# Down projections of a decoder trunk in five rounds of half-size block products

## Chip, cores and metric

The kernel runs on one core of one Trainium2 chip. The metric is the device time of one execution in microseconds (us), lower is better; it is the median of several runs. Two versions of the kernel are compared on the same chip. The engines are named as in the profile: PE is the matrix engine (TensorE), DVE the vector engine, ACT the scalar engine, POOL the GpSimd engine, SP the engine whose queue issues most DMAs. SBUF is the on-chip memory, PSUM the eight accumulator banks of PE.

## What is computed

The reference is a decoder trunk of two layers on one sequence of 1024 tokens and 1024 features: a short-convolution layer, then a layer of dilated attention over shared keys and values. Each layer ends with a gated feed-forward block of inner size 2816, and each part is normed before and after:

```python
def _swiglu(x, w_in, w_out):
    gate, up = jnp.split(x @ w_in, 2, axis=-1)
    return (jax.nn.silu(gate) * up) @ w_out

for layer in range(DEPTH):                       # DEPTH = 2
    g = norm_g[layer]
    xn = _rms_norm(x, g[0])
    if layer < N_A:
        mix = _short_conv(xn, conv_in_w[layer], conv_w[layer], conv_out_w[layer])
    else:
        if shared is None:
            shared = _shared_kv(x, kv_norm_g, kv_w)
        mix = _dilated_attention(xn, q_w[j], o_w[j], shared, slopes)
    x = x + _rms_norm(mix, g[1])
    ff = _swiglu(_rms_norm(x, g[2]), ffn_in_w[layer], ffn_out_w[layer])
    x = x + _rms_norm(ff, g[3])
```

The change concerns `(...) @ w_out`, the down projection: 1024 tokens by 2816 inner features times 2816 by 1024, once in each layer. All data is float32.

## The kernel before

**Precision.** PE multiplies in a rounded format, so each float32 factor is split into a high and a low part: ACT copies it with rounding (`*_hi`), DVE subtracts that from the original (`*_lo`). A product is three matmuls: high x high, high x low, low x high.

**Phases.** They follow each other as `PHASES` lists them: `conv_in`, `conv_out`, `norm1`, `up0`, `down0`, `norm2`, `attn`, `oproj`, `norm3`, `up1`, `down1`, `norm4`. Each engine has one program, written out by hand in its order; semaphores (`Signal` objects, one count for each phase) let engines wait for each other. There is no scheduler: an instruction that waits holds up everything behind it on its engine.

**Up projection (`up0`, `up1`).** It already computes each pair of column blocks as seven products of sums of blocks. For each of 22 sets POOL makes four sums of weight blocks (L1971), ACT and DVE split them (L1083, L1506), PE runs 7 products of 12 matmuls of 128x512 (L741), and DVE adds the results out of the banks. The inner features go to DRAM (`hid_spill`).

**Down projection (`down0`, `down1`).** The inner features are 22 tiles of 128. A unit is one tile `f` and one half of the tokens; the first 22 units serve tokens 0 to 511, the second 22 the rest. For each unit SP loads a 128x1024 block of `ffn_out_w` (`raw`, two buffers) and a 128x512 block of features back from DRAM (`hraw`). ACT and DVE split both (`w_hi`/`w_lo`, L1017 and L1400; `h_hi`/`h_lo`, L1185 and L1605). PE adds the unit to four token tiles, each in two banks: 4 x 2 x 3 = 24 matmuls (L770), 1056 in a layer. POOL has nothing to do for a unit.

**Norms.** After unit 22 the four token tiles of the first half are taken out of the banks: ACT squares them (L1065), DVE multiplies by the gain (L1472), POOL makes the inverse root (L1892, L1898), ACT scales and POOL and DVE add to the residual (L1118, L1935, L1480). This happens in `down_layer` between units of the second half. The last two units are done tile by tile, so that the norm of the second half starts with its first tile. After `down0`, in phase `norm2`, the normed tiles (`xn`, L1493) are transposed by PE (L639) and split (L1028, L1412) as the input of attention. POOL scales the first weight chunks of attention by the norm's gain (L1995).

The few lines of PE that the change replaces, in `down_layer`:

```python
passes = [(n, a, w) for n in units
          for a, w in ((h_hi, w_hi), (h_hi, w_lo), (h_lo, w_hi))]
for h in range(2):
    for i, (n, a, w) in enumerate(passes):
        mm = pe.matmul(bank(b + h), a[:, n % SPLIT_RING, t % HT * P:(t % HT + 1) * P],
                       w[:, a_slot(base + n), h * HALF:(h + 1) * HALF], ...)
```

## Time and profile before

| | us |
|---|---|
| median of 3 runs | 2508.31 |
| lowest and highest | 2507.82, 2512.53 |
| span of the profiled execution | 2505.2 |
| first down projection, about | 236.5 (844.5 to 1081.0) |
| from there to attention's last input | 25.9 (1081.1 to 1107.0) |
| second down projection, about | 239.1 (2257.5 to 2496.6) |
| end of the last down projection to the end | 8.6 |

How to read the profile: it is one execution. Busy time of an engine is the time in which it works on an instruction; a group of instructions is named by its line in the code, its engine, what it writes and reads, and its shape. "Idle before" an instruction is put down to what released it. Matmuls overlap in PE, so the time of a single one is longer than the distance to the next. In a row of the timeline the first number is the start and the second the duration; if another engine or a lock holds an instruction up after it has begun, that is inside its duration.

### The profile page before, as it was taken

How to read it: one execution, taken by the hardware profiler on the slowest of the kernel's cores; microseconds unless marked ns; L12 is line 12 of the kernel's file. 1: busy time of each engine (PE TensorE's matmuls, PEld its weight loads, DVE VectorE, ACT ScalarE, POOL GpSimd, SP SyncE). 2: the span in 40 equal slices, each digit the busy share in tenths (PEclk: the TensorE clock that was granted, in tenths of full speed). 3: DMA queues.
4: the chain of work that ended last, by engine and by line, in shares of the span. 5: the costliest groups of instructions: out<-in, count | busy, mean ns of one | idle time of the engine just before them, and what ended most of it. 6: DMA issues, size and time to landing. Idle time of an engine off the chain costs nothing.

```text
span 2505.2 us, 31211 instructions
## 1 busy us (share of the span) xinstructions
PE 2341.8 (93%) x10928; PEld 1939.1 (77%) x10928; DVE 1297.0 (52%) x1962; ACT 907.6 (36%) x1692; POOL 477.2 (19%) x542
## 2 busy tenths in 40 slices
PE   7999996999999999988898889879889999999998
PEld 5888784888888888866777777767668888888887
DVE  4333319655665434374555555563485565553443
ACT  3111116323232234343555555563442232332333
POOL 1000018222222001031111111100552222210011
PEclk9999997999999999999999999999889999999999
DMA  4111111233223444442323222222023223324444
GB/s 135 44 49 50 59 42 43 76 87 90 76 76 93 130 144 148 143 141 70 70 57 75 62 60 55 68 51 110 25 68 100 78 76 89 89 69 168 142 148 146
DMA packets 202209, 219.28 MB, mean 88 GB/s; under 512 B 13792, under 2 KB 153056, under 8 KB 200032
## 3 DMA queue, kind: packets, MB, share of 16 engines
q1 hardware_dynamic: 199136, 206.10, 28.1%
q10 hardware_dynamic: 2944, 11.53, 1.3%
q8 instruction: 72, 1.18, 0.2%
q14 instruction: 57, 0.47, 0.1%
HBM read 160.98 MB, written 31.46 MB: 77 GB/s over the span
## 4 chain that ended last, share of the span: by engine, by line
PE 84%; DVE 6%; ACT 3%; issue 3%; POOL 3%; DMA 1%; SPq 0%; DVEq 0%; ACTq 0%; POOLq 0%
PE banks L741 33%; PE banks L770 19%; PE banks L600 11%; PE banks L842 8%; PE banks L681 6%; PE banks L880 2%; PE banks L892 2%; PE banks L905 2%; POOL raw L1995 1%; PE banks L919 1%; ACT w_hi L1017 1%; DMA q_stack<-q_parts 1%; DVE w_lo L1400 1%; PE banks L639 1%; ACT scores L1349 1%
## 5 line engine op out<-in xcount | busy, mean ns | idle before, releaser
L741 PE MATMUL banks<-xb,up_split 128*128 128x512 f32 x3696 | 848.5, 392 | 11.9 <-DVE xb L1449 11.9
L741 PEld LDWEIGHTS banks<-xb,up_split 128*128 128x128 f32 x3696 | 699.8, 190 | 158.2 <-issue 12.4
L1400 DVE TENSOR_TENSOR w_lo<-raw,w_hi 128x1024 fp32r<-128x1024 f32 x152 | 188.2, 1239 | 434.1 <-ACT w_hi L1017 432.4
L1017 ACT CAST w_hi<-raw 128x1024 fp32r<-128x1024 f32 x152 | 159.1, 1049 | 451.2 <-PE banks L770 290.1
L770 PE MATMUL banks<-w_hi,h_hi 128*128 128x512 f32 x704 | 273.9, 389 | 0.0
L770 PE MATMUL banks<-w_hi,h_lo 128*128 128x512 f32 x704 | 273.9, 389 | 0.0
L770 PE MATMUL banks<-w_lo,h_hi 128*128 128x512 f32 x704 | 273.9, 389 | 0.0
L1506 DVE TENSOR_TENSOR up_split<-sums,up_split 128x512 fp32r<-128x512 f32 x176 | 154.1, 877 | 163.5 <-ACT up_split L1083 163.3
L1971 POOL TENSOR_TENSOR sums<-raw_up 128x512 f32<-128x512 f32 x88 | 115.1, 1310 | 395.9 <-DMA raw_up<-in_ffn_in_w 197.8
L770 PEld LDWEIGHTS banks<-w_hi,h_lo 128*128 128x128 f32 x704 | 132.1, 188 | 27.7
L770 PEld LDWEIGHTS banks<-w_hi,h_hi 128*128 128x128 f32 x704 | 132.1, 188 | 27.4
L770 PEld LDWEIGHTS banks<-w_lo,h_hi 128*128 128x128 f32 x704 | 132.1, 188 | 27.2
L1802 DVE TENSOR_TENSOR pt<-banks,pt 128x128 fp32r<-128x128 f32 (+7 forms) x128 | 96.9, 757 | 100.7 <-ACT pt L1293 100.0
L1083 ACT CAST up_split<-sums 128x512 fp32r<-128x512 f32 x176 | 108.5, 618 | 88.4 <-PE banks L741 86.9
L2031 POOL TENSOR_TENSOR resid<-o_parts 128x64 f32 (+1 forms) x128 | 46.9, 366 | 480.9 <-ACT o_parts L1309 480.9
L842 PE MATMUL banks<-x_hi,w_hi 128*128 128x512 f32 x384 | 112.6, 411 | 10.3 <-DVE x_lo L1412 6.2
L1506 DVE TENSOR_TENSOR up_split<-raw_up,up_split 128x512 fp32r<-128x512 f32 x132 | 116.4, 883 | 7.7 <-ACT up_split L1083 7.7
L842 PE MATMUL banks<-x_lo,w_hi 128*128 128x512 f32 x384 | 119.9, 413 | 0.0
L1786 DVE CUSTOM_DVE_ANT_0 scores<-banks,bias 128x128 f32<-128x128 f32 (+7 forms) x128 | 96.5, 754 | 36.9 <-PE banks L880 33.3
L880 PE MATMUL banks<-k_stack,q_stack 128*128 128x256 f32 (+1 forms) x382 | 94.2, 355 | 22.8 <-DVE neg_max L1786 13.3
L842 PE MATMUL banks<-x_hi,w_lo 128*128 128x512 f32 x384 | 114.1, 410 | 0.0
L1349 ACT ACTIVATE scores<-scores,neg_max 128x128 f32<-128x128 f32 (+7 forms) x128 | 99.8, 780 | 19.9 <-DVE neg_max L1786 19.5
(146 smaller groups left out, 3349.8 us busy)
## 6 DMA issues: line engine op xcount, KB each, us to landing
raw_up<-in_ffn_in_w SPq DMA_DIRECT2D x88, 512.0 KB, 5.4
raw<-in_ffn_out_w SPq DMA_DIRECT2D x88, 512.0 KB, 3.5
hid_spill<-hid SPq DMA_DIRECT2D x88, 256.0 KB, 2.5
hraw<-hid_spill SPq DMA_DIRECT2D x88, 256.0 KB, 3.5
k_stack<-k_parts SPq DMA_DIRECT2D x32, 512.0 KB, 6.3
raw<-in_conv_in_w SPq DMA_DIRECT2D x24, 512.0 KB, 3.8
raw<-in_kv_w SPq DMA_DIRECT2D x16, 512.0 KB, 3.9
q_stack<-q_parts SPq DMA_DIRECT2D x64, 128.0 KB, 2.3
```

What stands on the lines that cost most here:

```text
L600: mm = pe.matmul(bank(out_bank), w[:, slot, k * P:(k + 1) * P], a[:, k, h * HALF:(h + 1) * HALF], start=(i == 0), stop=(i == len(passes) - 1))
L681: mm = pe.matmul(bank(t), a(2 * q + k)[:, t * P:(t + 1) * P], w[:, slot, k * HALF:(k + 1) * HALF], start=(q == 0 and i == 0), stop=(last a ...
L741: mm = pe.matmul(bank(b_out), up_split[:, p, a, q * P:(q + 1) * P], xb[:, RIGHT_OF[p], b, q, :], start=(i == 0), stop=(i == len(passes) - 1))
L770: mm = pe.matmul(bank(b + h), a[:, n % SPLIT_RING, t % HT * P:(t % HT + 1) * P], w[:, a_slot(base + n), h * HALF:(h + 1) * HALF], start=(n ...
L842: mm = pe.matmul(bank(PROJ + h), w[:, a_slot(chunk0["attn"] + c), k * P:(k + 1) * P], a[:, k, h * HALF:(h + 1) * HALF], start=(i == 0), st ...
L880: mm = pe.matmul(psum[:, SCORE + lo // HALF, 0:hi - lo], att["q_stack"][:, e, i * P:(i + 1) * P], att["k_stack"][:, e, n, lo:hi], start=(n ...
L1017: act.copy(w_hi[:, a_slot(n), :], raw[:, s, :]).then_inc(hi_ready.sem, 1)
L1083: act.copy(up_split[:, p, 0, :], src).then_inc(up_hi.sem, 1)
L1349: act.activation(att["scores"][:, s % 2, 0:n], att["scores"][:, s % 2, 0:n], ACT.Exp, bias=neg_max[:, s % 2:s % 2 + 1], scale=-1.0, accum_ ...
L1400: dve.tensor_tensor(w_lo[:, a_slot(n), :], raw[:, n % RAW_RING, :], f32(w_hi[:, a_slot(n), :]), ALU.subtract) \
L1506: dve.tensor_tensor(up_split[:, p, 1, :], src, f32(up_split[:, p, 0, :]), ALU.subtract).then_inc(up_lo.sem, 1)
L1971: pool.tensor_tensor(sums[:, out_, :], a, b, op).then_inc(summed.sem, 1)
```

## The change

Two tiles of inner features, `2m` and `2m+1`, form a pair; there are 11 pairs. With the two halves of the tokens and the two halves of the output features a pair is a 2x2 by 2x2 block product, and the new code computes it as seven products of 128x512 sums instead of eight. In each product A is a sum or difference of feature blocks (128 features x 512 tokens), B one of weight blocks (128 x 512), and PE adds 4 token tiles x 3 matmuls = 12 of 128x512 into four banks. A layer has 77 products, in five rounds:

| round | products | sums on POOL | sums on DVE | banks |
|---|---|---|---|---|
| 1, q = 0 to 21 | M3, M5 in turn | 1 each | none | 0 to 3, 4 to 7 |
| 2, q = 22 to 43 | M1, M4 in turn | 2 for M1 | 1 for M4 | the same |
| 3, q = 44 to 54 | M7 | 1 | 1 | 4 to 7 |
| 4, q = 55 to 65 | M2 | 1 | none | 4 to 7 |
| 5, q = 66 to 76 | M6 | 2 for even q, 1 for odd | 1 for odd q | 0 to 3 |

Each product is made in a fixed order: sums (POOL and DVE, `block_sums`, `right_sum`) into one of two buffers `down_sums`; rounding (ACT, `split_high`); subtraction (DVE, `split_low`) into one of three buffers `down_split`; then PE. POOL's sum for product q waits until DVE has split product q-2, ACT's rounding until PE has done product q-3. Where both factors are sums, ACT and DVE treat them as one operation of 1024 columns, otherwise as two of 512.

Between the rounds the banks are read. ACT copies M3, M5 and M1 out; DVE adds M4, M7, M2 (twice) and M6 to the four result blocks in `acc_tile`; POOL adds up C12 in SBUF. The first half's tokens are complete after round 3, and their norm is laid between the products of rounds 4 and 5. In the first layer their transposes, splits and the first scaled chunk of attention weights are laid there too; before, the transposes came at the end of the phase. The last three products are run tile by tile, once all three are split.

The inner features are loaded back from DRAM once for each block and stay in SBUF (`hid_tile`). Weights come as 128x512 blocks into 12 buffers (8 in round 5). Some attention buffers have other addresses. The up projection is unchanged except in its last set, where the first splits of the down projection stand.

The diff, cut to its core:

```diff
+    def product(self, q):
+        n = self.pairs
+        if q < 2 * n:
+            return (M3, M5)[q % 2], q // 2
+        if q < 4 * n:
+            return (M1, M4)[q % 2], (q - 2 * n) // 2
+        if q < 6 * n:
+            return (M7, M2)[q // n - 4], q % n
+        return M6, 7 * n - 1 - q
...
+    def pool_makes(self, q):
+        p, m = self.product(q)
+        return (1, 1, 2, 0, 1, 1, 2 - m % 2)[p]
+
+    def dve_makes(self, q):
+        p, m = self.product(q)
+        return (0, 0, 0, 1, 1, 0, m % 2)[p]
...
+                def tile_product(q, i):
...
+                    side = down_split[:, q % DOWN_RING]
+                    passes = ((0, 0), (0, 1), (1, 0))
+                    for j, (a, b) in enumerate(passes):
+                        mm = pe.matmul(bank(b_out), side[:, a, 0, i * P:(i + 1) * P], side[:, b, 1, :],
+                                       start=(p in (M3, M5, M1, M2) and first and j == 0),
+                                       stop=(last and j == len(passes) - 1), skip_group_check=True)
...
+                pe.wait_ge(*down_lo.at(ph, 2 * QN))
+                for i in range(HT):
+                    for q in range(QN - 3, QN):
+                        tile_product(q, i)
...
+                for q in range(DOWN_RING, QN):
+                    right_sum(ph, q + 1)
+                    split_low(ph, q)
+                    for t in range(HT):
+                        if q == 44:
+                            add_m4(t)
+                        elif q == 56:
+                            sum_c11(t)
+                        elif q == 67:
+                            add_m2(t)
+                        if q == 60 + t:
+                            gain_first(t)
+                        if q == 62 + t:
+                            right_added(norm_ph, t)
+                        if pre and q == (72, 73, 75, 76)[t]:
+                            low_part(norm_ph, t)
+                    if pre and q == 74:
+                        prepare(chunk0["attn"])
...
+                for q in range(QN):
+                    block_sums(ph, q)
+                    for t in range(HT):
+                        if q == 25:
+                            sum_c12(t)
+                        if q == 60 + t:
+                            inverse_root(square1, mean1, rstd1, t, sq1_done, mean1_done, rstd1_done,
+                                         norm_ph)
+                        if q == 63 + t:
+                            left_added(norm_ph, t)
```

**DVE in the middle of the down projection.** Before, for units of the second half: `raw` and `hraw` are the loaded weights and features.

```order
L1400 TENSOR_TENSOR w_lo<-raw,w_hi 128x1024
L1605 TENSOR_TENSOR h_lo<-hraw,h_hi 128x512
L1480 SCALAR_TENSOR_TENSOR resid<-acc,rstd,resid 128x640
L1400 TENSOR_TENSOR w_lo<-raw,w_hi 128x1024
L1605 TENSOR_TENSOR h_lo<-hraw,h_hi 128x512
```

Now, at the end of round 4 and the start of round 5 (`down_sums` is a sum, `down_split` its split, `acc_tile` a result block):

```order
L1855 TENSOR_TENSOR down_split<-down_sums_89,down_split 128x512
L1857 TENSOR_TENSOR down_split<-down_raw,down_split 128x512
L1710 SCALAR_TENSOR_TENSOR resid<-acc_tile_81,rstd,resid 128x640
L1967 TENSOR_TENSOR acc_tile_83<-acc_tile_83,g_post 128x1024
L1855 TENSOR_TENSOR down_split<-down_sums_88,down_split 128x512
```

```order
L1860 TENSOR_TENSOR down_split<-down_sums_89,down_split 128x1024
L1950 TENSOR_TENSOR acc_tile_84<-banks,acc_tile_84 128x512
L1954 TENSOR_TENSOR acc_tile_84<-acc_tile_84,banks 128x512
L1950 TENSOR_TENSOR acc_tile_85<-banks,acc_tile_85 128x512
L1954 TENSOR_TENSOR acc_tile_85<-acc_tile_85,banks 128x512
L1950 TENSOR_TENSOR acc_tile_86<-banks,acc_tile_86 128x512
L1954 TENSOR_TENSOR acc_tile_86<-acc_tile_86,banks 128x512
L1950 TENSOR_TENSOR acc_tile_87<-banks,acc_tile_87 128x512
L1954 TENSOR_TENSOR acc_tile_87<-acc_tile_87,banks 128x512
L1871 TENSOR_TENSOR down_sums_89<-down_raw 128x512
L1860 TENSOR_TENSOR down_split<-down_sums_88,down_split 128x1024
```

The gain and the reads of the banks stand now between splits that PE waits for, and sums stand among them.

**POOL during the norm of the first half.** Before:

```order
L1935 TENSOR_TENSOR resid<-resid,acc 128x384
L1892 TENSOR_SCALAR mean<-square 128x1
L1898 TENSOR_TENSOR rstd<-mean,neg_half 128x1
```

Now, at the same work (end of round 4, start of round 5; `hid_tile` is a block of inner features):

```order
L2251 TENSOR_TENSOR resid<-resid,acc_tile_82 128x384
L2300 TENSOR_TENSOR down_sums_88<-hid_tile_78 128x512
L2303 TENSOR_TENSOR down_sums_88<-down_raw 128x512
L2208 TENSOR_SCALAR mean<-square 128x1
L2214 TENSOR_TENSOR rstd<-mean,neg_half 128x1
L2251 TENSOR_TENSOR resid<-resid,acc_tile_83 128x384
L2300 TENSOR_TENSOR down_sums_89<-hid_tile_76 128x512
```

POOL's sums for the products stand now between the operations of the norm.

## Rows read from the trace of the kernel before

**Rows 1.** The page: span, busy time and share by engine, and the chain by engine.

```profile
span 2505.2 us, 31211 instructions
...
PE 2341.8 (93%) x10928; PEld 1939.1 (77%) x10928; DVE 1297.0 (52%) x1962; ACT 907.6 (36%) x1692; POOL 477.2 (19%) x542
...
PE 84%; DVE 6%; ACT 3%; issue 3%; POOL 3%; DMA 1%; SPq 0%; DVEq 0%; ACTq 0%; POOLq 0%
```

**Rows 2.** Windows: length, busy of PE, PEld, DVE, ACT, POOL; clock, DMA share, GB/s.

```profile
844.50:1081.00 236.50, 236.50 (x1045) 195.76 (x1044) 96.69 (x104) 79.48 (x110) 16.25 (x26) 1.00 0.44 147
1081.00:1106.00 25.00, 17.89 (x101) 14.65 (x99) 20.56 (x19) 16.66 (x24) 10.93 (x17) 0.93 0.09 28
2257.50:2496.60 239.10, 239.10 (x1056) 197.83 (x1055) 95.37 (x101) 75.90 (x104) 12.43 (x20) 1.00 0.44 149
2496.60:2505.20 8.60, 0.24 (x2) 0.00 (x0) 5.29 (x4) 2.23 (x4) 3.68 (x5) 0.65 0.53 215
426.00:844.00 418.00, 418.00 (x1835) 345.85 (x1836) 253.31 (x350) 127.34 (x223) 112.45 (x90) 0.99 0.28 83
```

**Rows 3.** Groups of the page: busy us, mean ns of one, idle before.

```profile
L770 PE MATMUL banks<-w_hi,h_hi 128*128 128x512 f32 x704 | 273.9, 389 | 0.0
```

**Rows 4.** Timeline of the up projection: start us, duration us, engine, line, operation.

```profile
611.33 1.29 POOL L1971 TENSOR_TENSOR sums<-raw_up 128x512 f32<-128x512 f32 x1 [3.43 <-DVE up_split L1506]
611.77 1.40 DVE L1506 TENSOR_TENSOR up_split<-sums,up_split 128x512 fp32r<-128x512 f32 x1
...
441.89 1.30 POOL L1971 TENSOR_TENSOR sums<-sums,raw_up 128x512 f32<-128x512 f32 x1 [0.63 <-DVE up_split L1506]
442.00 0.69 DVE L1658 TENSOR_TENSOR third_gate<-third_gate,banks 128x512 f32<-128x512 f32 x1 [0.19 <-PE banks L741]
```

**Rows 5.** Timeline where DVE and POOL both have work queued.

```profile
427.80 1.73 POOL L1971 TENSOR_TENSOR sums<-raw_up 128x512 f32<-128x512 f32 x1
428.31 1.77 DVE L1506 TENSOR_TENSOR up_split<-raw_up,up_split 128x512 fp32r<-128x512 f32 x1
429.49 1.73 POOL L1971 TENSOR_TENSOR sums<-raw_up 128x512 f32<-128x512 f32 x1
...
411.32 1.28 POOL L1942 TENSOR_TENSOR xb<-t,xb 128x512 fp32r<-128x512 f32 x1
411.72 1.97 DVE L1489 SCALAR_TENSOR_TENSOR xn<-resid,rstd,g_pre 128x1024 f32<-128x1024 f32 x1
```

**Rows 6.** Timeline of the first down projection, during the first half's norm.

```profile
977.34 1.01 POOL L1935 TENSOR_TENSOR resid<-resid,acc 128x384 f32<-128x384 f32 x1 [13.78 <-ACT acc L1118]
977.40 1.50 DVE L1605 TENSOR_TENSOR h_lo<-hraw,h_hi 128x512 fp32r<-128x512 f32 x1
```

**Rows 7.** Durations of the operations, ns min/median/max, with first and last start.

```profile
L1400 DVE TENSOR_TENSOR w_lo<-raw,w_hi x152: 1214/1225/2772, 19.7 to 2481.7; 128x1024 fp32r<-128x1024 f32 x152
L1506 DVE TENSOR_TENSOR up_split<-sums,up_split x176: 676/687/1783, 402.3 to 2240.3; 128x512 fp32r<-128x512 f32 x176
...
L1017 ACT CAST w_hi<-raw x42: 1043/1048/1054, 853.2 to 1073.1; 128x1024 fp32r<-128x1024 f32 x42
```

**Rows 8.** DMAs of the down windows: KB and us to landing; GB/s in 40 slices.

```profile
hraw<-hid_spill SPq DMA_DIRECT2D x42, 256.0 KB, 3.5
...
GB/s 214 234 213 132 132 139 154 172 163 165 133 133 133 132 132 141 154 157 179 154 100 175 132 132 132 139 145 171 162 171 125 145 132 132 132 138 343 136 0 69
```

**Rows 9.** Timeline of `norm1`: a power of one column on POOL and DVE's addition.

```profile
376.00 0.55 POOL L1898 TENSOR_TENSOR rstd<-mean,neg_half 128x1 f32<-128x1 f32 x1
376.19 0.88 DVE L1480 SCALAR_TENSOR_TENSOR resid<-mix_conv,rstd,resid 128x640 f32<-128x640 f32 x1
```

**Rows 10.** Timeline of `norm2`, after PE's last down matmul.

```profile
1081.20 1.02 ACT L1065 ACTIVATE junk<-banks 128x1024 bf16<-128x1024 f32 x1 [1.10 <-PE banks L770]
...
1095.81 1.90 POOL L1995 TENSOR_TENSOR raw<-raw,gains 128x1024 f32<-128x1024 f32 x1
...
1105.75 1.22 DVE L1412 TENSOR_TENSOR x_lo<-banks,x_hi 128x1024 fp32r<-128x1024 f32 x1 [1.04 <-ACT x_hi L1028]
```

More of the change, by code:

```diff
@@ new lines, in load_ffn @@
+                    if n < FT - 1:
+                        store_hidden(up, n)
+                for m in range(NP - 4, NP):
+                    for i in range(2):
+                        load_block(down, layer, 2 * m + i, 2 * m + i, 1)
+                        load_hidden(layer, 2 * m + i, 2 * m + i, 1)
+                for m in range(NP):
+                    c = 2 * NP + 3 * m
+                    load_block(down, layer, c, 2 * m, 0)
+                    load_hidden(layer, c, 2 * m + 1, 2)
+                    load_block(down, layer, c + 1, 2 * m + 1, 1)
+                    load_block(down, layer, c + 2, 2 * m + 1, 0)
```

784 lines of the change are left out of this document (528 added, 256 removed).

## The prediction

> **What bounds the kernel now.** The page comes first: TensorE (PE) is busy for 93% of the span, and the chain of waits spends 84% in it [rows 1]. So a removed matmul counts in full, unless something else becomes late. Then the windows by stage: PE has no idle time in either down projection, and leaves it only after the first (25.0 us with 17.89 busy) and at the end [rows 2]. There 1045 matmuls take 236.50 us, 0.2264 us each; the 389 ns of a single one overlap [rows 2, 3]. VectorE (DVE) is busy for 40% of a down window and GpSimd (POOL) for 7%, so by busy shares alone all their new work would be hidden. The next view speaks against that.
>
> The timeline of the up projection shows DVE and POOL stopping each other. A DVE subtraction of 512 columns with both inputs in SBUF takes 0.69 us alone, and 1.40 us when it starts during a POOL operation: it ends 0.55 us after that one [rows 4, 7]. Beside the next POOL operation, a DVE operation that reads a PSUM bank keeps its 0.69 us [rows 4]. Where both engines have work queued they alternate, and one POOL and one DVE operation of 512 columns come every 1.69 us [rows 5]. I call what they share the port. It is held for 0.55 us by a DVE operation of 512 columns, 1.14 by a POOL one (1.69 - 0.55), and 1.09 by a DVE one of 1024 (411.72 + 1.97 = 413.69, 1.09 after POOL's end at 412.60) [rows 5]. So it is held some 0.13 us shorter than a DVE operation lasts alone, and 0.15 shorter than a POOL one. Before the change the port is lightly used in a down projection: 44 times 1.09 + 0.55 is 72 us of 239.
>
> **What is removed.** A layer has 1056 down matmuls, and after it 77 products of 12, 924. That is 132 x 0.2264 = 29.9 us a layer, **59.8 us** in all, if PE stays as full. One product lasts 12 x 0.2264 = 2.717 us.
>
> **What is added, round by round.** For each product both factors are split, and POOL and DVE make the sums. Port time against PE time:
> - M3 and M5, 11 pairs: 2 POOL sums and 4 DVE halves, 2 x 1.14 + 4 x 0.55 = 4.5 us of 5.43. Hidden.
> - M1 and M4, 11 pairs: 2.3 + 1.09 + 3 x 0.55 = 5.0 of 5.43. Hidden, but closely: POOL waits until the buffers of two products ago are split, and its queue also takes four sums of C12 at the round's start, 4 x 1.2 us. Bounds for both first rounds are 0 and 5 us a layer (0.4 for each pair if DVE's halves come ahead of POOL's sums); I take 2.
> - M7, 11 products: 1.14 + 0.55 + 1.09 = 2.78 us each, with the step from DVE's end to POOL's start (0.08) about 2.85, against 2.717. Ahead of it DVE adds four tiles from the banks, and behind it four more, before which M2 may not write: DVE takes them behind two further splits. I reckon 3 us lost (bounds 2 and 5).
> - M2, 11 products: 1.14 + 1.10 = 2.24, hidden at first, and DVE gets its lead of about 2.8 us back. From the sixth product on, the first half's norm is laid between them: four multiplications by the gain (1024 columns, now from SBUF and not from a bank, 1.09 each), four additions of 640 columns on DVE (0.88 alone, 0.75 held [rows 9]), four of 384 on POOL (1.01 alone, 0.86 held [rows 6]). I lay the queues beside each other, first come first served: from the split of the sixth product to that of the first M6 product 26.5 us pass (six splits, one sum on DVE and seven on POOL, which works two products ahead, and these twelve operations: 6.6 + 0.6 + 8.0 + 10.8 = 26.0, and the steps from engine to engine). PE has 16.3 us of work there and a lead of 3: 7 us lost.
> - M6, 11 products: six have two POOL sums, five one POOL and one DVE sum; a pair is 3 x 1.14 + 2 x 1.09 + 0.55 = 6.15 us against 5.43. I follow the queues. The second split comes 1.8 us behind the first. Then DVE takes eight operations of 512 columns from M2's banks (8 x 0.61 = 4.9 us), one sum (0.6) and the next split (1.15), while PE has 2.7 us of work: 4 us lost at one place. Four pairs at 5.9 to 6.3 us follow, since a sum must go POOL (1.29), ACT (1.05), DVE (1.22) before the next can start [rows 4, 7]. Last, PE runs three products tile by tile and starts when all three are split, 8.15 us. In all 1.8 + 6.7 + 24.4 + 8.15 = 41 us from the first product's start, against 11 x 2.717 = 29.9: 11 us lost (bounds 6 and 15).
>
> A layer therefore loses 2 + 3 + 7 + 11 = 23 us. The first layer adds a second norm in the same place: 1.9 us to scale a weight chunk on POOL, its split (1.09), and ACT's squares and scalings behind which the next split waits. DVE's four reads of the transposed tiles come from banks and fit in its waits. 5 us more (bounds 2 and 9). Reloading the inner features at the start may cost 0.5 us a layer: they land in 3.5 us [rows 8], PE needs them 8 us later. Sum **52 us**, bounds 20 and 75.
>
> **POOL's small operations, a rule weighed.** In the trace a power of one column takes 0.55 us on POOL, and a DVE addition that starts 0.19 us into it still takes 0.88 us [rows 9]; so I count its port time as nothing. The Trainium skill, page "SBUF — State Buffer", section "SBUF: two separate sides", says the shared pair is an exclusive lock held for the whole instruction. By that the twelve powers in these rounds would hold the port too, and the time would be 2500 and not 2493; the two rows of this case speak against it for so small an operation.
>
> **After the first down projection.** From PE's last down matmul (1081.1) to the last input of attention (1105.75 + 1.22 = 1107.0) pass 25.9 us [rows 10]. In that chain lie four splits of the first half's tiles and one chunk's scaling and splitting (1.90 + 1.05 + 1.22) [rows 7, 10]; the new code does these before PE ends. The second half's chain, down to the transposes that share banks, stays. I take **-6 us** (bounds -12 and 0), and -2 for two of four transposes that fall into PE's holes. At the very end the last tile's bank is read twice instead of once, in shorter operations, and tiles come every 2.04 instead of 2.72 us: **+0.5** on 8.6 us [rows 2].
>
> **Transfers.** A layer moves 154 blocks of 256 KB, 39 MB, in 209 to 235 us: 170 to 190 GB/s. The queues carry 147 at a share of 0.44, and 214, 234 and 343 GB/s in single slices of 6 us [rows 2, 8]. Twelve buffers cover some 11 us of lead against 3.5 us of landing. Hidden, at nothing; without that cover see rival B. The moved attention buffers change no instruction: nothing.
>
> **Sum.** The profiled execution has a span of 2505.2 us, 3.1 below the median of the runs. -59.8 + 52 - 8 + 0.5 = -15.3, so 2508.3 - 15.3 = **2493 us**.
>
> **Rivals.**
> - A, the port doesn't matter. For it: busy shares are low, and in the up projection DVE and POOL stop each other in every set of products while PE stays full [rows 2, 4], since products there wait with a lead. Against it: rounds M7 and M6 need more port time than PE time, and no lead survives eleven products. Time: all matmuls saved, with 0 to 20 us of loss: 2442 to 2470.
> - B, transfers become the bound and the kernel gets slower. Place: the rounds' loads, all in one queue. If they stayed at the 149 GB/s of now, a layer would take 39.4 MB / 149 = 264 us instead of 239, and the kernel 2508 + 50 - 8 = 2550. It decides from where less than 165 GB/s flows (39.4 / 239). The slices of 214 and more speak against it.
> - C, the waits chain worse than I follow. If DVE's halves always go ahead of POOL's sums, a pair in the first rounds needs 5.85 us, and M6 7 us or more: 65 to 75 us lost, 2506 to 2516.
> - D, POOL's powers hold the port for as long as they last, twelve times 0.55 us: 2493 + 6.6 = 2500. The addition of 0.88 us speaks against it [rows 9].
>
> **How the numbers follow.** Forecast 0.48 (2478 to 2503), D 0.10. A with the stretch up to 2478: 0.17. C: 0.17, of which three quarters lies within 0.2% of the time before and the rest above. B: 0.08. A measurement of this kernel can tell 0.2%, 5 us, from no change. Faster (below 2503.3): 0.48 + 0.10 + 0.17 less 0.03 for the upper edge of D, 0.72; within: 0.03 + 0.13 = 0.16; slower: 0.04 + 0.08 = 0.12. The range leaves out B and the lower half of A: 2462 to 2514.
>
> **What would show it.** Right: in the windows of the down projections PE has its idle time after the fourth product round starts, released by DVE's splits, some 20 us a layer; DVE's split of 1024 columns has a mean well above 1.22 us, and POOL's sums above 1.29; the first half of each window is full. The step at 1081 to 1107 is shorter by 6 us. Wrong: PE without idle time (A); POOL's or ACT's waits ended by loads of down_raw (B); idle time from the first round on (C). The weakest term is M6's 11 us, since it hangs on who goes first at the port.

## The result, and the profile after

The changed kernel takes **2557.95 us** (median of 4 runs, 2555.90 to 2559.78), the kernel before beside it 2508.07 us (median of 4). The ratio is 1.0191, with a 95% interval from 1.0177 to 1.0205: slower by 1.9%. The forecast was 2493 us, and its range ended at 2514. The profiled execution has a span of 2554.7 us against 2505.2 [rows 1].

The windows answer to [rows 2]. Columns are the stretch, its length, the busy time and instructions of PE, PEld, DVE, ACT and POOL, the granted clock, the DMA share and GB/s. The first six rows are the first down projection (rounds 1 to 4, round 5 up to its last three products, and those three), the seventh is the stretch behind it, and the last six are the second down projection.

```profile
844.90:914.10 69.20, 63.64 (x265) 51.48 (x265) 36.56 (x49) 29.34 (x52) 32.41 (x28) 0.95 0.60 206
914.10:982.00 67.90, 63.70 (x265) 48.39 (x264) 59.88 (x47) 24.29 (x35) 41.39 (x26) 1.00 0.46 155
982.00:1018.00 36.00, 33.03 (x133) 24.06 (x133) 34.56 (x28) 15.07 (x19) 20.44 (x13) 1.00 0.73 247
1018.00:1055.90 37.90, 32.69 (x132) 25.52 (x132) 31.87 (x31) 22.13 (x38) 30.91 (x27) 0.95 0.13 44
1055.90:1095.40 39.50, 29.17 (x129) 23.34 (x129) 29.38 (x27) 20.78 (x27) 32.69 (x23) 0.89 0.41 134
1095.40:1106.10 10.70, 10.70 (x37) 8.69 (x38) 6.17 (x8) 3.15 (x9) 7.89 (x11) 0.77 0.00 1
1106.10:1133.70 27.60, 15.54 (x57) 12.26 (x55) 15.39 (x17) 11.19 (x18) 11.68 (x16) 0.75 0.12 40
2290.00:2359.20 69.20, 62.72 (x266) 50.79 (x266) 36.46 (x49) 29.38 (x53) 31.95 (x24) 0.95 0.58 205
2359.20:2427.10 67.90, 63.65 (x266) 48.40 (x264) 59.86 (x47) 24.24 (x35) 41.38 (x26) 1.00 0.48 155
2427.10:2463.00 35.90, 32.88 (x132) 23.98 (x133) 34.45 (x28) 15.06 (x19) 20.36 (x13) 1.00 0.74 248
2463.00:2500.40 37.40, 32.40 (x132) 25.53 (x132) 32.99 (x31) 17.66 (x30) 29.35 (x23) 0.95 0.13 44
2500.40:2534.30 33.90, 23.05 (x97) 17.75 (x97) 26.19 (x22) 11.83 (x17) 26.55 (x17) 0.94 0.47 171
2534.30:2544.10 9.80, 9.80 (x36) 7.70 (x36) 4.80 (x7) 2.84 (x8) 7.85 (x10) 0.84 0.00 0
```

With PE full a round of 22 products takes 22 x 2.717 = 59.8 us and one of 11 takes 29.9. No round is full, and the loss begins in the first one. From PE's first to its last down matmul the first layer takes 261.2 us (full: 209.2) and the second 254.1; before, it was 241.3 and 239.5, read in the same way. The 49.5 us of difference between the spans lie as follows: first down projection +19.9, second +14.6, the stretch between them +12.2 (1171.7 to 1183.9), the end +2.2 (8.3 to 10.6), the start +0.6.

From the page of the changed kernel, the groups that answer to [rows 3]: PE's down matmuls, ACT's copy and DVE's subtraction of a whole product's sums (busy us, mean ns of one, idle time before and what ended it).

```profile
L964 PE MATMUL banks<-down_split 128*128 128x512 f32 x1848 | 454.6, 403 | 57.9 <-DVE down_split L1860 29.6
L1375 ACT CAST down_split<-down_sums 128x1024 fp32r<-128x1024 f32 x66 | 69.4, 1052 | 167.3 <-POOL down_sums L2291 77.9
L1860 DVE TENSOR_TENSOR down_split<-down_sums,down_split 128x1024 fp32r<-128x1024 f32 x66 | 113.1, 1713 | 30.5 <-ACT down_split L1375 30.1
```

PE stands for 57.9 us in the two layers together, where before it stood for none. DVE's operation of 1024 columns takes 1713 ns in the mean; before, one of this size had a median of 1225 [rows 7]. A chain can be read here: PE waits for DVE, DVE for ACT, ACT for POOL.

### Three places

**The start of the first round.** The waits of SP, in whose queue all loads stand (total, times, longest), and PE's idle times in the timeline:

```profile
SPq L558 <- DVE hid L1887: 11.9, 1, 11.9
```

```profile
848.53 3.02 PE L964 MATMUL banks<-down_split 128*128 128x512 f32 x12 [0.60 <-DVE down_split L1846]
852.36 5.73 PE L964 MATMUL banks<-down_split 128*128 128x512 f32 x24 [0.80 <-DVE down_split L1841]
862.25 5.06 PE L964 MATMUL banks<-down_split 128*128 128x512 f32 x11 [4.16 <-DVE down_split L1841]
```

The store of the last hidden tile (`store_hidden`, L558) stands in SP's queue after the second pair's loads. It waits 11.9 us for a tile that DVE multiplies only behind the first splits, and all loads from the third pair on stand behind it. PE runs dry three times, and the granted clock is at its half level, 1.2 GHz, from 861.4 on:

```profile
861.40:868.20 6.80, 5.95 (x14) 4.70 (x15) 5.46 (x6) 1.86 (x4) 4.40 (x3) 0.50 1.05 394
```

**Round 2.** The timeline of one pair M1 and M4 (start, duration; in brackets the idle time before and what ended it):

```profile
957.21 0.68 DVE L1850 TENSOR_TENSOR down_split<-hid_tile,down_split 128x512 fp32r<-128x512 f32 x1
957.46 1.57 POOL L2289 TENSOR_TENSOR down_sums<-hid_tile,hid_tile 128x512 f32<-128x512 f32 x1 [2.66 <-DVE down_split L1860]
957.81 1.77 DVE L1852 TENSOR_TENSOR down_split<-down_sums,down_split 128x512 fp32r<-128x512 f32 x1
959.00 1.74 POOL L2291 TENSOR_TENSOR down_sums<-down_raw 128x512 f32<-128x512 f32 x1
959.72 1.57 DVE L1871 TENSOR_TENSOR down_sums<-down_raw 128x512 f32<-128x512 f32 x1
960.84 1.05 ACT L1375 CAST down_split<-down_sums 128x1024 fp32r<-128x1024 f32 x1 [3.84 <-POOL down_sums L2291]
962.00 1.23 DVE L1860 TENSOR_TENSOR down_split<-down_sums,down_split 128x1024 fp32r<-128x1024 f32 x1 [0.72 <-ACT down_split L1375]
963.40 1.58 POOL L2289 TENSOR_TENSOR down_sums<-hid_tile,hid_tile 128x512 f32<-128x512 f32 x1 [2.66 <-DVE down_split L1860]
```

It is a ring: POOL's two sums (3.28 us from start to end, with two DVE operations taking turns at the port), ACT's copy 1.05, DVE's subtraction 1.23, and POOL again. From 957.46 to 963.40 pass 5.94 us; PE needs 5.43. POOL may not go ahead, since there are two buffers of sums and M1's is free only when it is split. POOL stands 2.66 us of each turn, and DVE waits .72 before its subtraction, so neither is full.

**Round 3.** One product M7:

```profile
988.59 0.69 DVE L1871 TENSOR_TENSOR down_sums<-down_raw 128x512 f32<-128x512 f32 x1
988.63 1.80 POOL L2294 TENSOR_TENSOR down_sums<-hid_tile 128x512 f32<-128x512 f32 x1 [1.26 <-DVE down_split L1860]
989.20 2.32 DVE L1860 TENSOR_TENSOR down_split<-down_sums,down_split 128x1024 fp32r<-128x1024 f32 x1
991.65 0.69 DVE L1871 TENSOR_TENSOR down_sums<-down_raw 128x512 f32<-128x512 f32 x1
```

The period is 3.06 us. DVE's sum holds the port to about 989.14 (.55), POOL's sum ends at 990.43 (1.29 later), DVE's split at 991.52 (1.09), and DVE starts again .13 later, because its next sum goes into the buffer that this split has just read and waits for the split's semaphore.

### The profile page after: what moved, and what is told of

The parts are those of the page before. It is cut to its first block, busy times and chain, and to the rows that moved or that the text cites. A ratio compares the mean times of both kernels' runs of the same rounds, so it can differ in the third digit from the quotient of the medians.

```text
span 2554.7 us, 31486 instructions
## 1 busy us (share of the span) xinstructions
PE 2322.6 (91%) x10664; PEld 1899.9 (74%) x10664; DVE 1490.2 (58%) x2118; ACT 956.2 (37%) x1802; POOL 782.1 (31%) x732
## 4 chain that ended last, share of the span: by engine, by line
PE 68%; DVE 11%; POOL 8%; issue 5%; ACT 5%; DMA 2%; SPq 0%; DVEq 0%; POOLq 0%; ACTq 0%
PE banks L913 32%; PE banks L764 10%; PE banks L1009 8%; PE banks L853 6%; PE banks L964 5%; DVE down_split L1860 3%; PE banks L1059 2%; PE banks L1047 2%; PE banks L1072 2%; ACT down_split L1375 1%; POOL down_sums L2291 1%; POOL down_sums L2289 1%; POOL raw_second L2401 1%; PE banks L1086 1%; POOL down_sums L2303 1%
## 5 line engine op out<-in xcount | busy, mean ns | idle before, releaser
L964 PE MATMUL banks<-down_split 128*128 128x512 f32 x1848 | 454.6, 403 | 57.9 <-DVE down_split L1860 29.6
L964 PEld LDWEIGHTS banks<-down_split 128*128 128x128 f32 x1848 | 351.2, 193 | 159.2 <-DVE down_split L1860 52.2
L1009 PE MATMUL banks<-x_hi,w_second 128*128 128x512 f32 x768 | 226.9, 414 | 5.7 <-ACT v_t L1507 3.3
L764 PE MATMUL banks<-x_hi,w_first 128*128 128x512 f32 x768 | 184.4, 392 | 7.8 <-DVE x_lo L1648 7.8
L764 PEld LDWEIGHTS banks<-x_hi,w_first 128*128 128x128 f32 x768 | 145.0, 189 | 38.4 <-issue 5.7
L1009 PEld LDWEIGHTS banks<-x_hi,w_second 128*128 128x128 f32 x768 | 138.4, 196 | 28.3 <-issue 6.3
L2117 DVE TENSOR_TENSOR pt<-banks,pt 128x128 fp32r<-128x128 f32 (+7 forms) x128 | 96.9, 757 | 100.4 <-ACT pt L1535 99.7
L1375 ACT CAST down_split<-down_sums 128x1024 fp32r<-128x1024 f32 x66 | 69.4, 1052 | 167.3 <-POOL down_sums L2291 77.9
L1860 DVE TENSOR_TENSOR down_split<-down_sums,down_split 128x1024 fp32r<-128x1024 f32 x66 | 113.1, 1713 | 30.5 <-ACT down_split L1375 30.1
L1009 PE MATMUL banks<-x_lo,w_second 128*128 128x512 f32 x384 | 120.9, 416 | 0.0
L1909 DVE TENSOR_TENSOR second_up<-first_up,banks 128x512 f32<-128x512 f32 x44 | 30.2, 687 | 138.1 <-PE banks L913 138.1
```

Of the source, the lines that this page charges most:

```text
L764: mm = pe.matmul(bank(out_bank), w_of[:, w, k * P:(k + 1) * P], a[:, k, h * HALF:(h + 1) * HALF], start=(i == 0), stop=(i == len(passes) - 1))
L964: mm = pe.matmul(bank(b_out), side[:, a, 0, i * P:(i + 1) * P], side[:, b, 1, :], start=(p in (M3, M5, M1, M2) and first and j == 0), stop ...
L1009: mm = pe.matmul(bank(PROJ + h), w_split(chunk0["attn"] + c)[:, w, k * P:(k + 1) * P], a[:, k, h * HALF:(h + 1) * HALF], start=(i == 0), s ...
L1860: dve.tensor_tensor(low, both[:], high, ALU.subtract).then_inc(down_lo.sem, 2)
L2117: dve.tensor_tensor(att["pt"][:, s % 2, 1, 0:n], two_banks(PROB)[:, 0:n], f32(att["pt"][:, s % 2, 0, 0:n]), ALU.subtract) \
```

## The experiments

Round times below go from the first matmul of a round to that of the next, in both layers (first / second). "Ratio" is to the kernel before, run beside each on the same chip (its median was 2511 to 2513 us in these sets); brackets are 95% intervals. Of each diff the core is shown; dots stand for the other lines.

| kernel | us, ratio | round 1 | 2 | 3 | 4 | 5 to the end |
|---|---|---|---|---|---|---|
| full PE | | 59.8 | 59.8 | 29.9 | 29.9 | 29.9 |
| changed | 2557.95, 1.0191 | 69.2 / 69.1 | 67.9 / 67.9 | 35.9 / 35.9 | 38.0 / 37.4 | 50.2 / 43.7 |
| later store | 2543.63, 1.0126 [1.0102, 1.0150] | 62.0 / 62.0 | 67.9 / 68.0 | 35.9 / 35.9 | 39.1 / 39.1 | 49.3 / 43.7 |
| third buffer | 2538.87, 1.0109 [1.0082, 1.0135] | 69.0 / 68.0 | 64.9 / 64.9 | 32.9 / 32.9 | 38.1 / 39.1 | 42.6 / 40.8 |
| tiny sums | 2496.66, 0.9934 [0.9913, 0.9955] | 66.3 / 65.1 | 59.8 / 59.8 | 30.7 / 30.7 | 30.2 / 30.5 | 43.6 / 37.5 |
| sums unread | 2537.79, 1.0102 [1.0072, 1.0133] | 68.8 / 66.2 | 62.0 / 62.4 | 35.8 / 35.7 | 37.5 / 39.0 | 46.3 / 43.4 |
| three edits | 2525.19, 1.0060 [1.0041, 1.0078] | 61.6 / 61.6 | 64.9 / 64.9 | 32.9 / 32.9 | 38.9 / 39.1 | 44.2 / 40.7 |
| and tiny norm | 2509.50 (one run) | 62.3 / 61.6 | 64.9 / 64.8 | 32.9 / 32.9 | 30.0 / 30.0 | 45.5 / 41.9 |
| DVE's sums | 2520.19, 1.0043 [1.0029, 1.0058] | 69.2 / 69.3 | 60.8 / 60.8 | 31.3 / 31.3 | 33.8 / 33.9 | 48.3 / 43.9 |
| with store, end | 2503.45, 0.9967 [0.9956, 0.9979] | 62.0 / 62.0 | 60.8 / 60.8 | 31.3 / 31.3 | 33.9 / 33.9 | 47.0 / 44.2 |

### The store in SP's queue

```diff
                             load_hidden(layer, 2 * m + 1, 2 * m + 1, 1)
-                            if m == 1:
+                            if m == 4:
                                 store_hidden(up, n)
```

> The changed kernel with one line moved: the last hidden tile's store (two DMAs that wait for the product of that tile) stands three pairs later in SP's queue. In the changed kernel SP waits 11.9 us in it (L558) with the loads of the third pair and later behind it, and PE stands .60, .80 and 4.16 us in the first round and runs 6.83 us at half clock after it. Theory that this head-of-line wait causes the first round's loss: round 1 falls from 69.2 us to 62 to 65 (full PE 59.8), both layers together give 8 to 14 us: 2544 to 2550. Rival, the queue's own speed or the sums pace round 1: it stays at 69 us and the time at 2556 to 2560.

Round 1 fell from 69.2 to 62.0 us in both layers, and the span by 13.1 us. The window shows the clock back at full and the queue no slower than before:

```profile
845.40:907.30 61.90, 60.56 (x264) 49.47 (x265) 44.13 (x49) 29.86 (x52) 35.19 (x28) 1.00 0.67 230
```

So the wait of 11.9 us behind the store costs 7.2 us a layer. It is one cause, with its size; by the medians the kernel gains 14.3 us, just more than the 8 to 14 expected.

### A third buffer for the sums

```diff
-        down_sums = [at(212, "down_sums0", [2, HALF]), at(40, "down_sums1", [2, HALF])]
+        down_sums = [at(212, "down_sums0", [2, HALF]), at(40, "down_sums1", [2, HALF]),
+                     at(44, "down_sums2", [2, HALF])]
...
-                both = down_sums[q % 2]
+                both = down_sums[q % 3]
...
-                    pool.wait_ge(*down_lo.at(ph, 2 * (q - 1)))
+                    pool.wait_ge(*down_lo.at(ph, 2 * (q - 2)))
```

> The changed kernel with a third buffer for the sums (44 KB, free there), so that POOL and DVE may write a sum two products ahead instead of one. Theory that a ring through two buffers (POOL sum, ACT copy, DVE low half, back to POOL) sets the pace of rounds 2 to 5: round 2 falls from 67.9 to 60 to 62 us, rounds 3 and 4 by 2 to 4 us each, both layers give 20 to 30 us: 2528 to 2538. Rival, the shared port: the same POOL and DVE work still has to pass it one after the other, round 2 stays above 66 us and the time at 2552 or more.

The time lies just past the ring theory's upper end, far from the rival's. But only a part of what it said of the rounds came true. Round 3 fell by 3.0 us as expected. Round 4 did not fall (38.1 and 39.1 us, where 2 to 4 us less were expected). Round 5 gained most, 7.6 us in the first layer and 2.9 in the second. Round 2 lost 5.1 us instead of 8.1 (expected: at most 2.2), and where it loses has changed. In its steady part POOL's first sum starts at 958.17 and 963.61, and PE has no idle time:

```profile
958.17 1.60 POOL L2290 TENSOR_TENSOR down_sums<-hid_tile,hid_tile 128x512 f32<-128x512 f32 x1 [1.60 <-DVE down_split L1853]
963.61 1.59 POOL L2290 TENSOR_TENSOR down_sums<-hid_tile,hid_tile 128x512 f32<-128x512 f32 x1 [1.60 <-DVE down_split L1853]
```

That is 5.44 us, PE's own pace. What is left is one gap at the round's start (and the clock behind it, 0.97 for the round), where POOL first makes the four C12 sums (7.46 us beside DVE's work), with further sums of M1 behind them in its queue:

```profile
914.65 7.46 POOL L2315 TENSOR_TENSOR acc_tile<-acc_tile,acc_tile 128x512 f32<-128x512 f32 x4 [1.24 <-ACT acc_tile L1415]
929.10 1.33 PE L965 MATMUL banks<-down_split 128*128 128x512 f32 x3 [3.15 <-DVE down_split L1861]
```

### Port or ring: sums of 8 columns, and sums that nobody reads

In the first kernel POOL's sums keep their places and waits and lose their length; in the second they keep length and place, but ACT doesn't wait for them (loads that overwrite what POOL reads wait for POOL instead).

```diff
+                w = slice(0, HALF if m == 0 else 8)
...
-                    pool.tensor_tensor(both[:, 0, :], hid_half(2 * m, 1), hid_half(2 * m + 1, 2), ALU.add) \
+                    pool.tensor_tensor(both[:, 0, w], hid_half(2 * m, 1)[:, w], hid_half(2 * m + 1, 2)[:, w], ALU.add) \
```

> The changed kernel with POOL's sums for the down products over 8 of 512 columns from the second pair of each round on (that part of the sums is left out). All waits and orders stay; POOL's use of the port and its share of the ring go. If the sums cause the rounds' loss in either way (port or ring), rounds 2, 3 and 4 come to within 2 us of full PE (59.8, 29.9, 29.9) and the time to 2470 to 2490. If the loads do, they stay as they are: 2550 or more.

```diff
-                both = down_sums[q % 2]
+                both = down_sums[q % 2] if m == 0 else own_sums
...
-                    act.wait_ge(*pool_sum.at(ph, plan.pool_sums(q)))
+                    if m == 0:
+                        act.wait_ge(*pool_sum.at(ph, plan.pool_sums(q)))
```

> The changed kernel with POOL's sums made in full but into a buffer that nobody reads, from the second pair of each round on (ACT and DVE split old contents: the sums are left out of the result), and ACT doesn't wait for them. The port carries all that it carried, the ring through POOL is cut. Port theory: rounds stay as they are, 2545 to 2558. Ring theory: rounds 2 to 4 within 2 us of full PE, as with tiny sums: 2470 to 2495.

```profile
911.20:971.00 59.80, 59.80 (x265) 49.54 (x264) 41.23 (x47) 24.91 (x35) 14.34 (x25) 1.00 0.57 182
971.00:1001.80 30.80, 30.26 (x134) 24.59 (x133) 22.44 (x27) 14.14 (x19) 7.61 (x12) 1.00 0.81 276
1001.80:1032.00 30.20, 30.12 (x132) 24.62 (x133) 25.38 (x31) 22.43 (x40) 18.89 (x26) 1.00 0.17 55
```

```profile
913.50:975.40 61.90, 60.60 (x265) 49.10 (x264) 59.58 (x47) 25.41 (x35) 42.03 (x26) 1.00 0.53 170
975.40:1011.20 35.80, 32.83 (x134) 23.97 (x133) 32.90 (x28) 14.83 (x19) 20.18 (x13) 1.00 0.75 249
1011.20:1048.70 37.50, 32.58 (x133) 25.84 (x134) 31.97 (x32) 23.08 (x40) 31.89 (x27) 0.95 0.13 45
```

The first fence is of the kernel with tiny sums (rounds 2, 3, 4): PE is full in round 2 and within .8 us of it in the others, with up to 276 GB/s from the queue. So POOL's sums, by port or ring, cost 61 us of the 97 that the two layers lose, and the loads cost nothing in these rounds. The time of 2496.7 is 7 us above what was expected (2470 to 2490); rounds 1 and 5 stay long, and round 5 still loses 13.7 and 7.6 us. The second fence is of the kernel with unread sums, whose time fell between the theories, and the rounds say why. Round 2 is a **ring**: cut it and 5.9 of 8.1 us come back, though DVE is as busy as before (59.58 us against 59.88). In rounds 3 and 4 nobody waits for POOL's sums any more, and they stay at 35.8 and 37.5: what holds them passes through the **port**. But in round 3 the port isn't alone. DVE's own sum still goes into one of two buffers here, and its period is 3.06 us as in the changed kernel. In the kernel with the third buffer it is 2.84, since the next sum starts before the split has ended:

```profile
990.89 0.68 DVE L1872 TENSOR_TENSOR down_sums<-down_raw 128x512 f32<-128x512 f32 x1
993.73 0.68 DVE L1872 TENSOR_TENSOR down_sums<-down_raw 128x512 f32<-128x512 f32 x1
```

So of the 6.0 us that round 3 loses, DVE's wait for its own buffer is 2.4 (11 times .22), the port's excess over PE's 2.717 us is 1.4, and 2.3 are the gap before round 4. With tiny sums the round takes 30.7 us: without POOL's time on the port, DVE's wait fits beside PE's work.

### The three edits together, and the norm in round 4

The third edit puts the first normalised tile behind the last C22 sum on DVE. In the changed kernel's timeline DVE stands 2.59 us at it, and the sum behind it, whose products PE ended at 1106.1, comes at 1110.56:

```profile
1106.62 0.68 DVE L1974 TENSOR_TENSOR acc_tile<-acc_tile,g_post 128x512 f32<-128x512 f32 x1
1109.89 0.75 DVE L1723 TENSOR_SCALAR acc_tile<-resid,rstd 128x1024 f32<-128x1024 f32 x1 [2.59 <-POOL rstd L2214]
1110.56 0.68 DVE L1961 TENSOR_TENSOR acc_tile<-banks,acc_tile 128x512 f32<-128x512 f32 x1
```

```diff
-                    if pre and i >= 2:
-                        normed(norm_ph, HT + i - 2)
+                    if pre and i >= 3:
+                        normed(norm_ph, HT + i - 3)
                 if pre:
+                    normed(norm_ph, TT - 2)
                     normed(norm_ph, TT - 1)
```

> The changed kernel with the later store, the third sums buffer, and one DVE step moved in the first down projection's end: the first normalised tile of the lower half (it waits for its root) stands behind the last tile's C22 sum instead of ahead of it; in the changed kernel DVE stood 2.59 us at that step with the sum behind it, whose bank was ready 4.5 us before. Late store gave 14 us and the third buffer 19 to 20 us by themselves. If they add up and the moved step gives 2 to 4 us: 2516 to 2524. If the late store's gain is eaten by the later rounds (what is loaded sooner is not needed sooner): 2528 to 2538. The stretch from the last down matmul to the last x_lo, 27.7 us in the changed kernel, should be 23.5 to 26 us.

It came 1.2 us above the first range. By the spans the two edits give 13.1 and 17.8 us, the moved step 3.1 of its stretch, and all three 35.8. By the medians it is 14.3 and 19.1, and 32.8 for all three. Within the scatter of some us they add up. The stretch from the last down matmul to the last `x_lo` fell from 27.5 to 24.4 us.

> The three edits, and of the norm's steps on the upper half of the tokens (rounds 4 and 5) the gain (DVE, 1024 columns), the right addition (DVE, 640) and the left addition (POOL, 384) cut to few columns: left out of the result. In full they take 4 x (1.21 + .87 + 1.09) = 12.7 us of DVE and POOL per layer. Theory that rounds 4 and 5 are bound by what DVE and POOL do one after the other on the port: they lose 8 to 12 us per layer together, 2498 to 2508. Rival, that they wait for the sums' ring or the squares' order: under 4 us per layer, 2514 or more.

Round 4 fell from 38.9 and 39.1 to 30.0 us: its whole loss is the upper half's norm and POOL's sums for M2 beside each other. 9 us come back there; round 5 takes 1.2 to 1.3 back, as its own work is no shorter, so a layer gains 6.9 and 8.0 us, at or just below the lower end of what was expected (8 to 12), and the one run of 2509.5 us lies 1.5 us above its range. With tiny sums, where the norm is full, round 4 is as short (30.2 and 30.5): either of the two by itself would fit, and only both together don't.

### The sums on DVE

```diff
-        return (1, 1, 2, 0, 1, 1, 2 - m % 2)[p]
+        return (1, 1, 0, 0, 0, 0, 0)[p]
...
-        return (0, 0, 0, 1, 1, 0, m % 2)[p]
+        return (0, 0, 2, 1, 2, 1, 2)[p]
```

The first line counts the sums that POOL makes for M3, M5, M1, M4, M7, M2, M6, the second DVE's; `right_sum` makes the left sum too where POOL has none.

> The changed kernel with the sums of rounds 2 to 5 all made by DVE, none by POOL; nothing else differs. A 128x512 sum takes DVE .55 to .68 us and POOL 1.09 to 1.30 us, and with nothing of POOL's beside them DVE's operations should all run at their undisturbed length: 4.5 us for a pair of round 2 (5.43 at full PE), 2.5 us for M7 and M6, 2.0 us for M2 (2.72). If the loss is POOL's time on the port and the ring through it: round 2 60 to 61 us, round 3 30.5, round 4 32 to 34, round 5 with the last three 36 to 40, 2510 to 2522. Rival, that DVE, now with all the work in one order, waits for ACT's copies in turn and becomes the bound: round 2 over 64 us and 2540 or more.

> The kernel with DVE's sums, and the later store and the moved step of the end. If all three add up: 2492 to 2504, a tie with the kernel before or faster. If DVE is the bound in rounds 2 to 5: 2522 or more.

The windows of the second kernel, rounds 2, 3, 4, 5 up to the last three:

```profile
907.00:967.80 60.80, 60.10 (x266) 49.44 (x265) 52.86 (x67) 24.97 (x35) 7.17 (x4) 1.00 0.56 180
967.80:999.10 31.30, 30.38 (x133) 24.53 (x132) 29.20 (x39) 14.08 (x18) 0.00 (x0) 1.00 0.75 257
999.10:1033.00 33.90, 31.15 (x133) 24.48 (x133) 32.20 (x42) 23.72 (x42) 16.12 (x19) 1.00 0.18 62
1033.00:1069.90 36.90, 27.87 (x128) 22.11 (x128) 36.33 (x41) 19.60 (x25) 14.52 (x10) 0.95 0.44 143
```

DVE does 20 operations more in round 2 and is busy for 7 us less (52.86, before 59.88): it no longer waits at the port inside them. Rounds 2 to 4 came within .8 us of what was expected, round 5 did not (48.3 and 43.9 us, expected 36 to 40). Its row says why for the first layer: DVE is busy for 36.33 of 36.90 us, so it is mostly DVE's own work that bounds it: 11 products of .60 + .60 + 1.14, eight additions from banks, and in the first layer four `x_lo` tiles and a weight split. With the later store and the moved step this is **faster than the kernel before**, by a third of a per cent: 2503.45 us, ratio 0.9967.

### What is left in rounds 4 and 5

Four more kernels build on that one: the first two on it, the third on the second, and the last has all edits.

```diff
-                    right_sum(ph, q + 1)
+                    right_sum(ph, q + 2)
```

> The kernel with DVE's sums, later store and moved end step, and with it the third sums buffer, DVE making its sums two products ahead instead of one. With DVE's sums round 2 came to 60.8 us, round 3 to 31.3, round 4 to 33.9, round 5 with the last three to 46.6 and 43.8. Theory that DVE's own busy time is what is left: nothing to gain, within 2 us of 2503. Rival, that DVE still waits for ACT's copies between a sum and its split: rounds 4 and 5 fall by 2 us or more each and the time to 2490 to 2497.

2499.94 us, ratio 0.9956 [0.9942, 0.9970]. Rounds 4 and 5 together went from 80.9 and 78.1 to 79.2 and 75.5 us. So both theories fell short: it is more than nothing, less than the rival's price.

```diff
-                        elif q == 56:
+                        elif q == 55:
                             sum_c11(t)
...
-                        if pre and q == (72, 73, 75, 76)[t]:
+                        if pre and q == (72, 73, 76, 76)[t]:
                             low_part(norm_ph, t)
-                    if pre and q == 74:
+                    if pre and q == 76:
                         prepare(chunk0["attn"])
```

> The kernel with DVE's sums, later store and moved end step; two more orders on DVE: in the first down projection the last two x_lo tiles of the upper half and the split of the next weights, three operations of 1.14 us, stand behind the last split instead of ahead of it (DVE stood 2.83 us idle there, waiting for PE); and the four C11 sums at the end of round 3 stand one split earlier. If DVE is the bound of rounds 4 and 5, the last split comes 2 to 3.4 us earlier in the first layer, and the gap at the start of round 4 (about 2.3 us in the changed kernel) closes to under 1 us in both layers, but what DVE gains there it also needs: 2498 to 2502 in all. If PE's end is set elsewhere: 2503 as before.

2501.09 us, 0.9959 [0.9946, 0.9972]. Round 3 fell from 31.3 to 30.6 us, and the first layer's round 5 from 47.0 to 43.8. Of those 3.2 us the stretch behind took 2.1 back (24.5 to 26.6 us to the last `x_lo`): the moved operations are needed there.

```diff
-                for q in range(QN - 3):
+                for q in range(QN - 2):
...
-                    for q in range(QN - 3, QN):
+                    for q in range(QN - 2, QN):
```

> As the kernel before it in this set, with the last two products instead of the last three computed tile by tile. Tile by tile, the PE starts only when the last split is there, so 8.15 us of matmul lie behind that split; with two it is 5.43 us, and the first tile is ready .68 us sooner. If the end is set by that PE work, 2 to 3 us less per layer: 2493 to 2497. If the norm's chain behind it (about 2.9 us of DVE and POOL per tile) sets the end, .5 to 1.5 us less per layer: 2497 to 2500.

2498.91 us, 0.9954 [0.9937, 0.9971]. The down projections end 1.4 and 4.2 us sooner, and what follows them takes 2.2 and 2.0 us longer (to the last `x_lo` 28.8 us; the end 12.6 instead of 10.5). The norm's chain, not PE's last tiles, sets the end. Three kernels show it in a row. PE finishes a last tile every 2.72 us before, 2.04 with three products and 1.36 with two, and the end takes 8.3, 10.5 and 12.6 us: three steps of .68 us (2.04) that PE gains come back behind it. In the changed kernel DVE's last three additions stand 2.95 and 2.92 us apart (2543.37, 2546.32, 2549.24), slower than PE's tiles.

> All that gave something: DVE's sums in rounds 2 to 5 with the third buffer and two products ahead (2499.9 by itself), the later store, the moved end step, the two orders on DVE and the last two products tile by tile (2498.9). If the third buffer's gain (1.5 to 3 us) is of the same waits as that of the last two products, nothing is added: 2497 to 2500. If they add up: 2493 to 2497. In either case faster than the kernel before by .5 to .8%.

2499.52 us (2496.72 to 2501.89), 0.9954 [0.9939, 0.9969]: nothing is added, as the first case said. The chain behind the products, DVE's own work and the first round's 1.8 us are what the rounds still show.

## Why the prediction was wrong

Term by term, both layers together. "Saved" is against the 480.8 us that the two down projections took before; 1.7 us of them are the 16 transposes that already stood in the first.

| term | forecast | measured |
|---|---|---|
| matmuls saved | -59.8 | -62.4 |
| rounds 1 and 2, with the reload | 5 | 35.1 |
| rounds 3 and 4 | 20 | 27.7 |
| round 5, with the second norm | 27 | 34.1 |
| between the down projections | -8 | +12.2 |
| start and end | +0.5 | +2.8 |

**Right.** 59.8 us of matmuls went, and PE's pace where it is fed is 0.2264 us a matmul as forecast (round 2 with tiny sums: 59.84 us for 264, 0.2267 each). What replaced them is port time, waits through ACT, and the norm in round 4. Transfers weren't the bound: 247 GB/s in round 3, 276 with tiny sums, where rival B feared 149. B's time of 2550 us is the nearest on record, but by luck: its mechanism, a full queue, isn't there. Rival A fell too, with idle time of PE in every round. (Its range of 2442 to 2470 has a small slip: by the prediction's own sum it is 2441 to 2461.) Idle time from the first round on was named as the sign of rival C.

**The step that failed: rounds 1 and 2, "hidden" and "hidden, but closely", 2 us a layer.** They lose 9.4 and 8.1, 30 us more than forecast in both layers. Two things were missed.
- Round 1 has little to do with sums. Reloading the features was priced by its landing (3.5 us) and not by the queue in front of it: 0.5 us forecast, 7.2 measured, with the clock's fall inside. The order of SP's queue was in the whole diff; following that queue past each instruction that waits would have found the store.
- Round 2's port sum of 5.0 us is not what sets its pace. The ring of 5.94 us is. The prediction had its parts: the wait for the buffer of two products ago, and a pair of 5.85 us "if DVE's halves always go ahead of POOL's sums" (rival C). It priced the first at nothing and kept the second as a bound, and did not follow one turn through ACT. The rest, about 2.5 us, falls at the round's start, where the four C12 sums stay in POOL's queue for 7.4 us, not 4.8.

**Round 3: mechanism right, size off.** 2.85 us a product forecast, 3.06 measured: the sum of POOL counted 1.14 us in saturation [rows 5], here 1.29, and DVE's wait for its own semaphore costs .13, where .08 were counted. The third buffer takes that wait out, and the period is 2.84. With the gap of 2.3 us before round 4, rounds 3 and 4 lose 14.2 and 13.5 us, forecast 10.

**Round 5.** Forecast 11 us, 16 in the first layer; measured 20.3 and 13.8. Even with tiny sums 13.7 and 7.6 remain. There PE stands 3.39 and 2.01 us behind DVE's eight additions, and 2.51 and 3.35 before the last three products, which wait for the last split. In the first layer some 3.3 us more are 32 transposes, which PE now does in this round: work that was moved, not lost. The rest isn't resolved.

**Norm behind the first down projection.** Forecast -8, measured +12.2. One part is a misread row: I took 1081.1 as PE's last down matmul, where the transposes begin between them; the last down matmul of before ends at 1085.66. So the chain to the last `x_lo` was 21.3 us, not 25.9, and there was less to win. It became 27.5, 6.2 longer. Of these the moved step gave 3.1 back, and some 2.0 are an estimate for PE's faster last tiles, of the same kind as at the end. The remaining 1 us is open.

The other 6.0 us lie between that `x_lo` and the second down projection, in code that the change hardly touches:

```profile
1107.00:1857.00 750.00, 647.59 (x3450) 538.67 (x3451) 414.98 (x844) 373.90 (x844) 158.17 (x224) 0.95 0.27 71
```

```profile
1133.70:1889.60 755.90, 649.88 (x3450) 541.02 (x3451) 415.29 (x843) 373.71 (x844) 159.38 (x224) 0.95 0.27 70
```

The first row is of before, the second of the changed kernel, up to the same matmul. The 5.9 us arise in it; the rest of the way takes 400.3 and 400.4 us. Over the whole stretch the granted clock is at half for 71.7 us before and 78.5 after, which is worth 3.4 us of PE; across the other kernels it is 71.7 to 85.3 us, whatever was edited. It can't be all: the kernel with unread sums has 71.7 us too, and takes 1155.6 us for the whole stretch, where before took 1150.3. The kernel before varies as much by itself: in its 40 later runs from 2505.99 us at a mean clock of .978 to 2516.73 at .972, and its profiled run, at .976, is one of the short ones. So whether the change costs anything here stays open.

**The end.** Forecast +0.5, measured +2.2, and 10.3 to 10.6 us in all kernels that end tile by tile over three products. The tiles of 2.04 us were in the forecast, but not that the chain behind them needs 2.9 us a tile, so that what PE gains there is lost behind it.

**The clock was not in the sum at all.** Before, no down projection had a stretch at half clock. After, there are 23.9 us in the first and 17 in the second, in seven pieces, and all seven begin during a wait of PE of 1.98 to 7.08 us or within 1.2 us of its end (the one at 861.40 during that of 4.16). But three waits of 1.91, 2.09 and 2.31 us in the same rounds had none behind them. At most half of it, some 20 us, is PE's loss; where DVE bounds the round it costs less, and it can't be added to the other terms.

In all the layers lose 52.0 and 44.9 us, 96.9, where 52 were forecast; 57.9 of them are idle time of PE, and the rest lies in the clock, the transposes and PE's start after each wait (at 852.36 the second matmul comes .34 us behind the first, where the distance is .23). With tiny sums 36 of them remain, so POOL's sums, by port and ring, are 61. Of the 36, 11.8 are in round 1, where the later store takes out its cause, and 21.3 in round 5.

## What to carry to other kernels

Busy shares and a count of port time give a lower bound for a round only. Follow one full turn of the dependency ring through its engines and buffers (POOL, ACT, DVE, back to POOL) and compare that with PE's pace; if the ring is longer, its period is the price for every turn. A second engine that shares a port was no help here, since it needs twice the port time for the same operation (1.1 to 1.3 us against .55): giving all sums from round 2 on to the busier, faster engine took some 38 us out. Each load that a change adds can have the wait of an instruction ahead of it in the queue as its price, and not only its landing time. And PE's last tiles may come faster than the chain behind them takes them; then shortening them moves time and saves none.

## What the runs showed of the hardware

A power of one column on POOL waits for the port but DVE doesn't wait for it. In the changed kernel's timeline, POOL's power takes .88 us and not .55 when it starts .22 us into a DVE operation, and DVE's multiplication of 1024 columns, started .39 us into the power's time, keeps its 1.21 us:

```profile
1029.93 0.68 DVE L1857 TENSOR_TENSOR down_split<-down_raw,down_split 128x512 fp32r<-128x512 f32 x1
1030.15 0.88 POOL L2214 TENSOR_TENSOR rstd<-mean,neg_half 128x1 f32<-128x1 f32 x1
1030.54 1.21 DVE L1967 TENSOR_TENSOR acc_tile<-acc_tile,g_post 128x1024 f32<-128x1024 f32 x1
```

The Trainium skill, page "SBUF — State Buffer", section "SBUF: two separate sides", has the shared pair as an exclusive lock for the whole instruction. The sums of 512 columns agree with that (alternation in the fence on round 2); for the power only the waiting half of it shows, and nothing speaks for rival D.

The time of one and the same kernel moves with the clock in long stretches: 40 runs of the kernel before lie between 2505.99 us (mean granted clock .978) and 2516.73 (.972). Differences of 3 us between these kernels rest on the rounds' times, not on the whole.
